# Sixteen experts in one order of size: five visits of 128 rows, three of 96 in 32-row units, eight of 64

## The reference

```python
sel = softmax(h @ w_router) + b_router            # 16 experts in 4 groups
best = group with the largest sum of its top two
idx = the two experts with the largest sel inside best
wts = scores[idx] / sum(scores[idx])
for e in range(16):
    act = silu(h @ w_gate[e]) * (h @ w_up[e])      # 1024 -> 512
    y += combine[:, e] * (act @ w_down[e])         # 512 -> 1024
x = x + g2 * y
```

## Time and profile before

| | us |
|---|---|
| median of 3 runs (1364.97 to 1373.53) | 1368.42 |
| profiled execution | 1364.29 |
| its span, first to last instruction | 1362.7 |
| mean granted TensorE clock | 0.921 |
| PE busy, share of the span | 84% |
| DMA, mean over the span | 258 GB/s |

### The profile page before, as it was taken

How to read it: one execution, slowest core, us unless ns; L and a number is a source line. 1 busy time by engine, 2 the same in 40 slices (tenths; PEclk the granted TensorE clock), 3 DMA queues, 4 the chain that set the end, 5 groups by cost and what they waited for, 6 DMA issues and landing times.

```text
span 1362.7 us, 15572 instructions
## 1 busy us (share of the span) xinstructions
PE 1146.1 (84%) x5660; PEld 620.9 (46%) x5660; DVE 448.3 (33%) x1059; ACT 252.4 (19%) x568; POOL 131.9 (10%) x230
## 2 busy tenths in 40 slices
PE   3885499999999399999986888779936999999990
PEld 0552245444444144445545777554424444444440
DVE  3656310111000371533157667331464011111105
ACT  2241001111101231111123444221110101111101
POOL 4100100000000300000112000210000000000002
PEclk8996599999999799999997899889966999999995
DMA  9996879999999567642424000836043999999945
GB/s 363 373 411 269 322 277 349 399 411 411 411 405 354 178 232 288 248 148 72 184 76 138 0 0 0 246 92 235 31 178 117 360 351 413 411 405 405 412 154 204
DMA packets 66927, 351.95 MB, mean 258 GB/s; under 512 B 6873, under 2 KB 8449, under 8 KB 54018
## 3 DMA queue, kind: packets, MB, share of 16 engines
q1 hardware_dynamic: 46944, 289.72, 54.8%
q0 software_dynamic: 16000, 55.53, 12.2%
q10 hardware_dynamic: 3938, 6.09, 1.2%
HBM read 326.75 MB, written 28.51 MB: 261 GB/s over the span
## 4 chain that ended last, share of the span: by engine, by line
PE 72%; DVE 11%; DMA 9%; issue 4%; ACT 2%; POOL 1%; ACTq 1%; SPq 0%; DVEq 0%; POOLq 0%
PE pb L892 19%; PE pb L1114 14%; PE pb L934 9%; PE pb L896 8%; DMA ring<-in_ada_w_dram 4%; PE pb L942 4%; PE pb L774 3%; PE pb L1216 2%; PE pb L886 2%; DMA hT_raw<-f_d 2%; PE pb L821 2%; DVE ring L2279 1%; DMA h<-h_d,idx 1%; PE pb L1193 1%; PE pb L1065 1%
## 5 line engine op out<-in xcount | busy, mean ns | idle before, releaser
L892 PE MATMUL pb<-ring,h 128*128 128x512 f32 x576 | 260.7, 603 | 4.2 <-DVE h L2039 4.2
L1114 PE MATMUL pb<-ring,hT_raw 128*128 128x512 f32 x512 | 231.4, 607 | 4.0 <-DVE ring L2140 2.3
L892 PEld LDWEIGHTS pb<-ring,h 128*128 128x128 f32 x576 | 107.4, 193 | 126.9 <-issue 126.9
L1114 PEld LDWEIGHTS pb<-ring,hT_raw 128*128 128x128 f32 x512 | 97.1, 194 | 123.2 <-issue 122.2
L2053 DVE COPY hT_raw<-pb 128x512 f32<-128x512 f32 (+1 forms) x32 | 22.1, 692 | 338.5 <-PE pb L934 203.2
L934 PE MATMUL pb<-ring,hT_raw 128*128 128x512 f32 x288 | 128.0, 597 | 0.0
L896 PE MATMUL pb<-ring,h 128*64 128x256 f32 x896 | 106.0, 384 | 0.0
L934 PEld LDWEIGHTS pb<-ring,hT_raw 128*128 128x128 f32 x288 | 53.6, 190 | 67.5 <-issue 67.5
L774 PE MATMUL pb<-ring,cT 128*32 128x512 f32 (+1 forms) x576 | 59.9, 554 | 26.7 <-DMA ring<-in_ada_w_dram 26.7
L896 PEld LDWEIGHTS pb<-ring,h 128*64 128x64 f32 x896 | 60.6, 137 | 42.2 <-issue 14.5
L666 POOL DMA_DIRECT2D ys_d<-hT_raw x32 | 18.2, 570 | 533.4 <-DVE hT_raw L2053 533.4
(11 more groups left out here) (329 smaller groups left out, 1261.1 us busy)
## 6 DMA issues: line engine op xcount, KB each, us to landing
ring<-in_w_down_dram SPq DMA_DIRECT2D x32, 2048.0 KB, 12.7
ring<-in_w_gate_dram SPq DMA_DIRECT2D x32, 2048.0 KB, 10.8
ring<-in_w_up_dram SPq DMA_DIRECT2D x32, 2048.0 KB, 11.5
ring<-in_ada_w_dram SPq DMA_DIRECT2D x24, 2048.0 KB, 10.2
ys_d<-hT_raw POOLq DMA_DIRECT2D x18, 512.0 KB, 8.3
ring<-in_kv_ada_w_dram SPq DMA_DIRECT2D x4, 2048.0 KB, 9.7
ring<-in_w_kvf_dram SPq DMA_DIRECT2D x4, 2048.0 KB, 13.0
h_d<-h ACTq DMA_DIRECT2D x8, 512.0 KB, 8.0
```

Of the source, the lines that this page charges most:

```text
L892: return T.matmul(bank[:, :], xgT[:, par, k, :], w[:, k * DE:(k + 1) * DE], start=(k == 0), stop=(k == KC - 1))
L1114: last = T.matmul(bank[:, :], hT[:, k, col[t]:col[t] + P], w[:, k * 512:(k + 1) * 512], start=(k == 0), stop=(k == KC - 1))
```

## The change

It has five parts. `FIXED` is 1: only expert 0 has a set place, all others are ordered by token count, largest first. The capacities are 128 rows for visits 0 to 4, 96 for 5 to 7 and 64 for 8 to 15. A 96-row visit works in units of 32 rows: each 32-row slice of the gathered rows is the stationary operand of four column tiles of 32, and each tile takes a quarter of the output columns; its result is stored by four DMAs. SP loads only expert 0 before the visit table, moves the fills forward, and loads expert 1's visit's gate after the table, then its up block once the gate block has landed; the `down` block follows with the next visit's gate. DVE makes the visit table directly behind the one-hot rows. On PE, 28 matmuls whose result nobody reads are added: ten ahead of the rank matmuls of layer 1, and in both layers ten ahead of and eight behind the slots' matmuls. The first eight visits are now written out, 8 to 13 are the loop.

```diff
+    FIXED = 1
+    NBIG, NMID = 5, 3
+    QUARTERS = [4] * NBIG + [3] * NMID + [2] * (NE - NBIG - NMID)
+    CAP = [QTR * q for q in QUARTERS]
+    STORES = [4 if q == 3 else 1 for q in QUARTERS]
...
                 def turn(v, par):
                     e = expert_of(v)
-                    before = expert_of(v - 1)
                     sp.wait_ge(E.gate, v + (e0 - 1))
                     load_weights(G_SLOT + par, wg_v, e, slot_loaded[G_SLOT + par])
-                    sp.wait_ge(E.down, 2 * v + (2 * e0 - 4))
-                    load_weights(D_SLOT + 1 - par, wd_v, before, slot_loaded[D_SLOT + 1 - par])
+                    if not (isinstance(v, int) and v - 1 < FIXED):
+                        before = expert_of(v - 1)
+                        if not (isinstance(v, int) and 2 * v + 2 * e0 == 4):
+                            sp.wait_ge(E.down, 2 * v + (2 * e0 - 4))
+                        load_weights(D_SLOT + 1 - par, wd_v, before, slot_loaded[D_SLOT + 1 - par])
...
-                order = (["d0", "g0", "g1", "u0", "d1", "u1"], ["u0", "d0", "u1", "g0", "g1"])[layer]
-                for kind, v in order:
-                    first(kind, int(v), e01[int(v)])
...
+                if FIXED:
+                    for kind in (("d", "g", "u"), ("u", "d", "g"))[layer]:
+                        first(kind, 0, 0)
+                        if layer == 0 and kind == "d":
+                            for r0 in range(MAIN, YROWS, SEQ):
+                                n = min(SEQ, YROWS - r0)
+                                sp.dma_start(ys_d[r0:r0 + n, :], x_prompt[0, 0:n, :]).then_inc(rows_filled, 16)
                 sp.wait_ge(perm_ready, layer + 1)
...
+                e = expert_of(1)
+                first("g", 1, e)
...
+                settled(G_SLOT + 1)
+                first("u", 1, e)
+                turn(2, 0)
                 turn(3, 1)
...
+                    for q in range(4):
+                        g.dma_start(rows_of.rearrange("(r t) (q n) -> q t r n", t=QTR, q=4)[q],
+                                    ysb[QTR * q:QTR * q + QTR, v % 2, 0:3 * D // 4].rearrange("t (r n) -> t r n", r=3)
+                                    ).then_inc(done, 16)
...
+            def spin(n):
+                for _ in range(n):
+                    T.matmul(pb[3][:, 0:2 * KC * NE], ident[:, :], wrf[:, :, :, :].rearrange("p k a e -> p (k a e)"),
+                             start=True, stop=True)
             def ranks(layer):
+                if layer:
+                    spin(10)
...
             def slots_to_tokens(layer):
+                spin(10)
                 pe.wait_ge(onehot_ready, layer + 1)
...
                 last.then_inc(idx_done, 1)
+                spin(8)
...
+                n = DE // 4
+                for r in range(3):
+                    for q in range(4):
+                        last = T.matmul(bank[QTR * q:QTR * q + QTR, n * r:n * r + n], xgT[:, par, k, QTR * r:QTR * r + QTR],
+                                        w[:, k * DE + n * q:k * DE + n * q + n],
+                                        start=first and r == 0, stop=final and r == 2, tile_position=(0, QTR * q))
...
+                if big == 3:
+                    n = D // 4
+                    for r in range(3):
+                        for k in range(KE):
+                            for q in range(4):
+                                last = T.matmul(pb[5 + r // 2][QTR * q:QTR * q + QTR, n * (r % 2):n * (r % 2) + n],
+                                                hactT_f[:, r * P + k * QTR:r * P + k * QTR + QTR],
+                                                w[:, k * D + n * q:k * D + n * q + n],
+                                                start=(k == 0), stop=(k == KE - 1), tile_position=(0, QTR * q))
```

More of the change, by code:

```diff
@@ L921, in pe_th @@
                 pe.wait_ge(S.hact, i + (b + 1))
-                for c in range(KE if big else KE // 2):
+                for c in range(big):
                     last = T.transpose(pb[2][:, c * P:(c + 1) * P], hact[:, c * P:(c + 1) * P], ident[:, :])
@@ L1917, in per_expert @@
                     return v.unsqueeze(1).unsqueeze(1).to_broadcast([P, 2, NT, NE])
-                key, order, small, visit, room, left = [e16[:, i, :] for i in range(6)]
+                key, visit, small, room, left = [e16[:, i, :] for i in range(5)]
                 t_rank, t_visit, t_room, t_ov, over, block_of, slot, col_of = [tokf[:, i, :] for i in range(8)]
@@ L1926, in places @@
                 tt(more, bc(key, NE, 1), bc(key, NE, 2), ALU.is_gt)
-                red(order, more, ALU.add)
-                link(V.tensor_scalar(small, order, float(NBIG), None, ALU.is_ge))
-                link(V.tensor_scalar(visit, order, 2.0, -2.0, ALU.mult, ALU.add))
-                link(V.scalar_tensor_tensor(out=visit, in0=small, scalar=3.0 - 2.0 * (NBIG - 1), in1=visit,
-                                            op0=ALU.mult, op1=ALU.add))
-                link(V.tensor_scalar(left, order, 0.0, 3.0, ALU.is_equal, ALU.mult))
-                tt(visit, visit, left, ALU.add)
+                red(visit, more, ALU.add)
                 of_token(t_visit, per_expert(visit))
```

174 lines of the change are left out of this document (96 added, 78 removed).

## The result

The changed kernel takes **1380.49 us** (median of 8 runs, 1377.06 to 1385.2); the kernel before takes 1367.28 (8 runs, 1358.47 to 1373.53). The ratio is 1.0106, interval [1.0081, 1.013]: about 1% slower. The forecast of 1338 is wrong, in its sign too. The profiled execution took 1381.35 us with a span of 1379.8, 17.1 us more than the span before.

What follows compares the result with a forecast made beforehand. PE set the pace in the two expert stages, with DMA nearly full. -12.1 - 2.4 - 2 x 6.7 = -27.9 took 1364.3 to 1336.4, plus 2 for the median: 1338 us, range 1316 to 1355.

Steps and rivals of the forecast that it cites:

- Start of layer 0: Before layer 0's expert stage: earlier VectorE tables and a shorter gather bring the first gate matmul forward 12.1 us, bounds -12.1 to -9.
- Start of layer 1: Before layer 1's expert stage: the same edit brings the first matmul 2.4 us forward; +1.6 if the gather waits for weights.
- "Nothing" for the fill's move: Before layer 0's stage: filling ys_d behind the first down block costs no time, as DMA had run dry there.
- Warming matmuls: On PE ahead of the expert stages: the added matmuls change nothing, 0 us, bounds -4.7 to +4.
- PE in the stage: In each layer's expert stage: smaller visits cut PE's time from 287.0 to 268.5 us, -18.5, if weights come in time.
- The dearer price that stood beside the sum: In 96-row visits: three column tiles giving 2.38 times would save 1.1 us a visit, not 3.1; whole 12 us slower.
- My slower rival: In 96-row visits: weight loads of 32-column matmuls show, +4 to +8 us a visit at half exposed, 1362 to 1386; chance 0.04.
- threshold of 4.7 us: In 96-row visits: exposed weight loads decide from 28 / 6 = 4.7 us a visit on.
- DMA in the stage: In each expert stage: late 64-row visits wait for weights, 6 x 3.8 = 22.8 us less 11 prefetched, +11.8, bounds 0 to +25.
- lead of 11 us: Before the last six 64-row visits: gate blocks land 9 to 12 us ahead of use, taken as 11, set against 22.8.
- DMA becomes the bound further down: In the stage's saturated tail: DMA at 360 GB/s makes a 64-row visit 18.9 us, a layer loses 10, total 1372; chance 0.08.
- signs of being wrong: In the expert stages: PE's waits begin in big visits, 96-row visits take as long as bigs, or no weight wait shows.

Runs made afterwards that it cites:

- the fill behind: The change with the fill of ys_d issued behind expert 0's gate and up blocks, as before the change, instead of behind its down block: 1381.04 us.
- half-load run: The change with gate and up blocks of visits 8 to 15 loaded by half, 1 MB instead of 2 MB each: 1329.77 us.
- the alternating kernel: The change with eight 128-row and eight 64-row visits in alternation, only expert 0 fixed and early: 1341.23 us.
- the two interleaved kernels: The change's own sizes, each of the first eight visits followed by a 64-row one: 1332.62 us; with the gather also ahead of the stores: 1328.03 us.

## Why the prediction was wrong, step by step

- **Start of layer 0 (-12.1): right.** From the rank matmuls to the first gate matmul 34.3 us became 22.3, -12.0. The absolute 154.3 and not 150.8 comes from ahead of it (+3.4). The releaser is VectorE's copy, as said, and its tables end at 153.40, as the forecast's 150.0 plus that delay. The gather was less clear of it than forecast: issued at 144.67 and landed at 151.37 (6.7 us, not 4.5), so that its transposes end at 153.45, at the same moment as the tables. And that it took 6.7 and not 17.45 us is owed to the fill's being done in time, for which the single early expert was enough (8.1 us with the fill behind) and, in the kernel before, the fill's move alone (6.3 us).
- **Start of layer 1 (-2.4): right in kind, smaller.** From the rank matmuls to the first gate matmul 23.57 us became 22.14, -1.4. The last to come is not VectorE's tables (1043.13) but the gather: issued at 1035.50, behind the gate block that SyncE issued at 1032.68, it lands at 1042.07, 6.6 us and not 4.5. The forecast had this as its bound (+1.6).
- **"Nothing" for the fill's move:** wrong in its place, nearly right in the sum. I looked for what it delays on its own queue and not at another engine that issues DMAs: ScalarE's third store of h_d took 9.32 us to issue, and PE's router product came 4 us later; at the rank matmuls 0.4 us of it was left against the run with the fill behind.
- **Warming matmuls (0): right**, shown by leaving them out. The first gate block took 10.09 us and not 8.91, with them as without (10.06).
- **PE in the stage (-18.5): a failed step, for the issue waits that it put at nothing.** Without weight waits a 64-row visit behind a 64-row visit takes 12.1 us and not 12.8 (the 12.8 was the difference of a pair), so the array would have given about 5 us more. The 96-row visit was 18.8 in my sum; without its waits they are cheaper than that (54.2 us between the downs of visits 4 and 7, where the forecast's prices give some 55.5; 18.4 from the down of visit 5 to that of visit 6). The dearer price that stood beside the sum, 1.1 us saved a visit, is not seen. But they wait for issue, 11.4 us in layer 0 and 10.1 in layer 1. The row I leant on the earlier trace rows had 384 short matmuls in one go; that the supply of instructions might not last over a whole visit was nowhere in the forecast. My slower rival had the right place and sign (the 96-row visits, +3.8 us each) and the wrong cause: PE stands in a few lumps of some 2 us, each until a packet of instructions is there, and not a little at each weight load; its threshold of 4.7 us was never reached.
- **DMA in the stage (+11.8, bounds 0 to 25): the other failed step, mis-sized.** Against the half-load run the stage has 299.0 - 275.1 = 23.9 us more, of which 1.7 are other issue waits: +22, near my upper bound. 17.0 of them are longer waits for blocks and rows (17.9 against 0.9), and some 3 are two down blocks that ran in 5.12 and 5.18 us where the others took 3.65, with a granted clock of 0.72 and 0.83 about them. I took a lead of 11 us at 411 GB/s against six short visits. With the measured rate and the measured visit, 391 GB/s and 12.1 us, the same sum gives 6 x (17.4 - 12.1) - 11 = +21: the mechanism was right, and both of its prices were too kind. Ahead of that DMA ran at a share of 0.89 for 166 us, since with five bigs in a row the ring is full and slots come free at PE's pace, and the end ran at 391 GB/s with stretches of 355 to 384. The 14.16 MB in 34.7 us of the earlier trace rows held because a big and a small visit average out within the ring's depth; sorting took that away.
- **Sum:** in layer 0 PE -25.7 (261.3 without waits or cold start, 287.0 before), DMA +22, issue +11.4, a colder start +1.2, and 0.9 for rows that the half-load run waits for too: +9.8, where +9.9 was measured. The forecast had -6.7: it lacks the 11.4 and 10 of the DMA term, and PE gave 7 more than it said.
- The rival "DMA becomes the bound further down" gave 1372 for a rate of 360 GB/s, by a stage of +10 us. The stage is indeed +10 us, but by another sum, so its nearness is luck: the end ran at 391 GB/s and not at 360, and the issue waits made the rest. It had 0.08. The Trainium skill, *DMA: Bandwidth & Descriptors*, Specifications, names some 358 GB/s as a limit of a core; the alternating kernel holds 408 GB/s over 200 us, so the traces don't bear that out, though single stretches of the sorted kernel lie there. That the rate was lower in those stretches stays unexplained.

Two of the signs of being wrong that had been named came: mids take as long as bigs (24.4, 23.1 and 16.0 us between the downs of visits 4 to 7, 21.2 on average), and PE's waits begin in a big visit (2.1 us ahead of the down of visit 4, for instructions). The waits for ring blocks came where they were forecast, from visit 10 on, but at 391 GB/s and not 411.

Shown are that PE stands until a 16 KB packet of instructions has come, that these waits follow the number of short matmuls close together, that a visit of longer matmuls between them removes most, and that neither tile shape, nor load traffic, nor straight-line code alone makes them. What stays open is what sets the moment at which a packet is asked for: in the change's layer 0 four of the five waits began 0.1 to 0.6 us after their packet had, and one 0.3 us before.

## What to carry to other kernels

When compute and transfer are nearly in balance, order the items so that each pair that fits in the buffers is balanced; sorting by size makes first the one idle and then the other, and a prefetch buffer only bridges its own depth. Count instructions per microsecond beside array time when a tile is cut into many short matmuls. And when a large DMA moves to another place, look at every engine that issues DMAs in that stretch, not only at its queue.

## What was not expected of the hardware

- A store's issue on ScalarE took 9.32 us (10.07 in the kernel before with the fill moved; 5.5 and 7.6 for the longest in the two interleaved kernels) while two DRAM-to-DRAM copies of 3.9 MB in all and a 2 MB block were under way; in the kernel before, without them, these issues take 0.32 to 0.93 us.
- Streams of 128-column matmuls in 32-row tiles (30 ns a record) ran 229 records in a row without a gap and then stood 2.3 us, until 1.4 us after a 16 KB packet of instructions; in all 11.4 us in the 66 from 254 to 320.
- In the half-load run the DMA share was 0.98 at 358 GB/s while PE waited for no weight block. A share near 1 alone doesn't tell that DMA bounds.
- The same router-to-rank stretch has an ada product of 7.0 to 9.7 us, from kernel to kernel (7.03, 8.32, 8.36, 9.52, 9.73), with a granted clock of 1.00 over the shortest and 0.72 over the longest; earlier work that ends sooner can meet the slower one and lose its gain.
